# Second power and first inverse step in one product, and token products of one head as transposes, in a chunked RWKV-7 recurrence

## What is computed

```python
def step(state, inp):
    r_t, w_t, k_t, v_t, kk_t, a_t = inp
    sa = jnp.einsum('bhvk,bhk->bhv', state, -kk_t)
    state = (state * w_t[:, :, None, :]
             + sa[..., None] * (kk_t * a_t)[:, :, None, :]
             + v_t[..., None] * k_t[:, :, None, :])
    return state, jnp.einsum('bhvk,bhk->bhv', state, r_t)
s0 = jnp.zeros((bsz, RWKV_HEADS, RWKV_HEAD_DIM, RWKV_HEAD_DIM), f32)
_, y = lax.scan(step, s0, tuple(map(seq_first, (r, decay, k, v, kk, a))))
```

## Time and profile before

| | |
|---|---|
| median of 3 runs | 2763.23 us (2763.11 to 2765.14) |
| profiled execution | 2771.98 us, of which the span is 2770.1 us |
| the stage `rwkv` on TensorE | about 1214.5 to 1765 us |
| granted clock of TensorE, mean | 0.986 of full |

### The profile page before, as it was taken

The page is one execution under the profiler, slowest core; times in us unless marked ns, Lnnn a source line. Parts: engine busy times, 40 slices in busy tenths (PEclk is TensorE's granted clock), DMA queues, the critical chain, the costliest instruction groups (busy, mean ns, idle before and its releaser), DMA issues. The chain is left out here.

```text
span 2770.1 us, 66149 instructions
## 1 busy us (share of the span) xinstructions
PE 2617.0 (94%) x28073; PEld 2190.7 (79%) x28073; DVE 1563.2 (56%) x2377; ACT 1318.0 (48%) x2272; POOL 316.2 (11%) x367
## 2 busy tenths in 40 slices
PE   6999999999999999989999999999999999999992
PEld 5989897777766766678999998888888888888882
DVE  4566664443035555544444444553326888888884
ACT  4645552222134444334444444552223777777771
POOL 0111222332000000001212121100001000000002
PEclk9999999999999999999999999999998999999996
DMA  4344332222132323313221201154345999999976
GB/s 111 148 167 145 125 138 89 92 93 74 37 96 65 99 68 102 114 38 81 55 69 52 64 21 33 48 152 129 121 185 219 397 395 395 395 396 395 395 301 258
DMA packets 162649, 440.53 MB, mean 159 GB/s; under 512 B 16295, under 2 KB 96825, under 8 KB 150097
## 3 DMA queue, kind: packets, MB, share of 16 engines
q1 hardware_dynamic: 146413, 381.95, 38.7%
q10 hardware_dynamic: 9060, 29.56, 2.8%
q0 software_dynamic: 6912, 25.17, 2.4%
HBM read 344.22 MB, written 92.41 MB: 158 GB/s over the span
## 5 line engine op out<-in xcount | busy, mean ns | idle before, releaser
L2671 DVE TENSOR_TENSOR ex_wL<-wx,ex_wH 128x2048 fp32r<-128x2048 f32 x192 | 436.1, 2286 | 46.5 <-ACT ex_wH L2575 43.8
L2575 ACT CAST ex_wH<-wx 128x2048 fp32r<-128x2048 f32 x192 | 366.4, 1912 | 96.3 <-PE ex_bank L2467 70.7
L2465 PE MATMUL ex_bank<-ex_wH,ex_xTH 128*128 128x512 f32 x512 | 199.4, 389 | 0.6 <-DVE ex_xTL L2676 0.6
L2467 PE MATMUL ex_bank<-ex_wL,ex_xTH 128*128 128x512 f32 x512 | 199.3, 389 | 0.0
L2466 PE MATMUL ex_bank<-ex_wH,ex_xTL 128*128 128x512 f32 x512 | 199.2, 389 | 0.0
L717 PE MATMUL ph_acc<-ph_wH,uH 128*104 128x512 f32 x480 | 191.5, 399 | 0.0
L717 PE MATMUL ph_acc<-ph_wH,uL 128*104 128x512 f32 x480 | 188.8, 393 | 0.0
L717 PE MATMUL ph_acc<-ph_wL,uH 128*104 128x512 f32 x480 | 188.6, 393 | 0.0
L419 PE MATMUL pf_acc<-uH,pf_wH 128*128 128x348 f32 x648 | 160.7, 356 | 6.4 <-DVE pf_wL L541 6.4
L419 PE MATMUL pf_acc<-uL,pf_wH 128*128 128x348 f32 x648 | 138.9, 323 | 0.0
L419 PE MATMUL pf_acc<-uH,pf_wL 128*128 128x348 f32 x648 | 138.3, 322 | 0.0
(11 more groups left out here) (416 smaller groups left out, 6879.5 us busy)
## 6 DMA issues: line engine op xcount, KB each, us to landing
wx<-in_expert_w_gate SPq DMA_DIRECT2D x32, 2048.0 KB
wx<-in_expert_w_up SPq DMA_DIRECT2D x32, 2048.0 KB
wx<-in_expert_w_down SPq DMA_DIRECT2D x32, 2048.0 KB
s_y<-ex_y ACTq DMA_DIRECT2D x32, 512.0 KB, 10.0
fw<-in_w_in SPq DMA_DIRECT2D x27, 512.0 KB
hw<-in_w_in SPq DMA_DIRECT2D x6, 2048.0 KB, 10.1
s_qkT<-ph_stg ACTq DMA_DIRECT2D x4, 2080.0 KB, 7.0
mb_gt<-s_pT SPq DMA_DIRECT2D x16, 512.0 KB, 3.6
```

The costliest lines, as they stand in the source:

```text
L2465: nc.tensor.matmul(out, aH, bH, start=first, stop=False)
L2467: return nc.tensor.matmul(out, aH, bL, start=False, stop=last)
L2575: nc.scalar.copy(wH[:, w, part], raw(j, s)[:, part]).then_inc(w_high, 1)
L2671: nc.vector.tensor_tensor(wL[:, w, part], raw(j, s)[:, part], wH[:, w, part], ALU.subtract).then_inc(w_low, 1)
```

## The change

Step 7 no longer issues the product with Q0 on its own. GpSimd writes its sum into the new middle place of `X2`, next to the second power, and one product with a moving operand twice as wide (104 columns) gives the next power and the product with the first factor, both into bank `bx`. ScalarE copies X4 from that bank as before, from columns 0 to 4 TC; VectorE's sum of step 7 reads columns 4 TC to 6 TC of the same bank and, new, waits for ScalarE's copy. GpSimd's sum waits for the step-7 sum of two chunks before instead of four. Of the token products those of the lower head (`h` = 0) are issued as transposes; those of the upper head stay.

```diff
-        X2 = sb("rw_X2", [128, 2, 2, 2, TC])
+        X2 = sb("rw_X2", [128, 2, 3, 2, TC])
...
-        Q0 = sb("rw_Q0", [128, TS4, 2, TC])
...
                 elif n == 7:
                     pe.wait_ge(*at_act(ch, 6))
                     pe.wait_ge(*at_pool(ch, 6))
+                    both = lambda e, h: bank[here(h), bx, 0:8 * TC].rearrange("p (k r t) -> p k r t", k=2, r=4)[:, :, e, :]
                     for e in range(2):
                         for h in range(2):
-                            mm(at(bx, 0, e, h), X2[here(h), ln, 1, e, :], X2[here(h), ln, 0, e, :], start=True, stop=True)
+                            mm(both(e, h), X2[here(h), ln, 2, e, :], X2[here(h), ln, 0:2, e, :], start=True, stop=True)
                         for h in range(2):
-                            mm(at(bx, 1, e, h), X2[here(h), ln, 0, e, :], X2[here(h), ln, 1, e, :], start=True, stop=True)
-                        for h in range(2):
-                            last = mm(at(bq, 0, e, h), X2[here(h), ln, 1, e, :], Q0[here(h), f, e, :], start=True, stop=True)
+                            last = mm(at(bx, 1, e, h), X2[here(h), ln, 0, e, :], X2[here(h), ln, 2, e, :], start=True, stop=True)
...
-                        last = mm(bank[here(h), 7, (2 * j + e) * RD:(2 * j + e + 1) * RD], src, c.ident[half(h), half(h)], start=True, stop=True)
+                        if h == 0:
+                            last = tr(bank[here(h), 7, (2 * j + e) * RD:(2 * j + e + 1) * RD], src, c.ident[half(h), half(h)])
+                        else:
+                            last = mm(bank[here(h), 7, (2 * j + e) * RD:(2 * j + e + 1) * RD], src, c.ident[half(h), half(h)], start=True, stop=True)
...
-                what = {6: (X2[0:PX, ln], four), 7: (X4[0:PX, ln], four), 8: (N8[0:PX, ln], two),
+                what = {6: (X2[0:PX, ln, 0::2], four), 7: (X4[0:PX, ln], four), 8: (N8[0:PX, ln], two),
...
-            for b, n in ((2, 4 * TC), (3, 2 * TC), (4, 4 * TC), (5, 2 * TC)):
+            for b, n in ((2, 6 * TC), (3, 2 * TC), (4, 6 * TC), (5, 2 * TC)):
...
-                    if ch >= TS4:
-                        pool.wait_ge(*at_dve(ch - TS4, 7))
-                    nc.gpsimd.tensor_tensor(Q0[0:PX, ch % TS4], M4[0:PX, ch % MS, :, 0, :], eye, ALU.add).then_inc(spool[ln], 1)
+                    if ch >= 2:
+                        pool.wait_ge(*at_dve(ch - 2, 7))
+                    nc.gpsimd.tensor_tensor(X2[0:PX, ln, 1], M4[0:PX, ch % MS, :, 0, :], eye, ALU.add).then_inc(spool[ln], 1)
...
                     if n == 7:
                         dve.wait_ge(*at_pool(ch, 6))
+                        dve.wait_ge(*at_act(ch, 7))
...
-                    tt(dst, pairs(bq), Q0[0:PX, ch % TS4] if n == 7 else Q[0:PX, ln, 1 - n % 2], ALU.add).then_inc(sdve[ln], 1)
+                    src = bank[0:PX, bx, 4 * TC:6 * TC].rearrange("p (e t) -> p e t", e=2) if n == 7 else pairs(bq)
+                    tt(dst, src, X2[0:PX, ln, 1] if n == 7 else Q[0:PX, ln, 1 - n % 2], ALU.add).then_inc(sdve[ln], 1)
```

## The result

The changed kernel takes 2913.05 us (median of 4 runs, 2906.97 to 2918.09) against 2764.18 us before: ratio 1.053, 95% interval 1.050 to 1.056. It is 149 us slower; 2743 us had been predicted. The profiled execution took 2918.09 us.

A forecast was written before the change was run, and what follows sets the result against it. The supply of TensorE's instructions was taken to bound two thirds of the stage. Fewer instructions -24.1, waits there +2.2, the other third +2.5: -19.4 us, taken as -20, from 2763.2 to 2743 us; likeliest case 2733 to 2751, range 2733 to 2768.

The forecast's parts named there:

- What bounds the kernel: In two thirds of the recurrence stage, TensorE's instruction supply: about 256 instructions per 3.97 us, against 3.54 us of work.
- the terms: Fewer TensorE instructions: 14 records a chunk, -24.1 us, of which step 7's eight give 13.8; array time adds 0.7 us.
- no supply bound: Rival: the "issue" gaps are a fixed toll per piece of instructions; +5.2 us, 2768 us; chance 0.13.
- Token products: Six of twelve products a chunk become transposes; a pair still takes 0.112 us, so array time saved is taken as zero.
- drain: Rival: each of 480 token transposes takes the array out of its quarters and back; +114 us, 2877 us; chance 0.07.
- The rule that I cited: On TensorE, a change of tiling mode drains it, and column tiling excludes float32 transposes; time as under drain, 2877 us.
- Serial: Rival: token transpose and product take turns on the array, 27 us of work; -4 us, 2759 us; chance 0.14 (or half).
- The new wait: VectorE's step-7 sum waits for ScalarE's X4 copy; step 8 0.12 us late, 10.0 us in all, mostly hidden by supply.
- The clock: In the recurrence stage, read at its full level of 2.4 GHz; the sum had no term for a change.

The follow-up runs named there:

- step7_order: Kernel before with the new step 7, token products as before, all waits kept but the one that ends last written first: 2758.08 us, ratio 0.9960.
- tokens_only: Kernel before with only the lower head's token products turned into transposes, step 7 unchanged: 2893.94 us, ratio 1.049.
- masked_split: Kernel before with each masked product of 104 columns issued as two of 52, 16 records a chunk more: 2789.28 us, ratio 1.0111.
- tokens_grouped: Kernel before with the lower head's token products as transposes, six in a row, then the upper head's six products: 2776.86 us, ratio 1.0038.
- the grouped runs: Kernel before with the lower head's token products as transposes, six or two in a row, then as many upper-head products: 2776.86 and 2810.26 us.

## Why the prediction was wrong

**What bounds the kernel** was read rightly. The supply of TensorE's instructions in pieces of 256 costs time: 16 records more a chunk gave +31 us where 30 were expected, and eight fewer, with no late wait, gave -16 where the terms make -14.5. The rival "no supply bound" falls.

**Token products** is the step that failed: "Array time saved: nothing", and the cost taken at nothing beyond it. Its direct term measured +138 us. The rival "drain" had the mechanism and the price: 0.306 us for each transpose, against 0.30 measured, from the norm's transposes of the earlier trace rows. I held it at 0.07 because the transposes into 16 partitions follow full-size ones without a toll. Those rows were the wrong witness: no product in a quarter stands near them, and what costs is the change between products in quarters and a transpose, in a quarter or full-size, which the earlier trace rows alone showed. The rule that I cited from the Trainium skill (TensorEngine Tiling (Array Packing), Key Properties and Restrictions) pointed the right way: the trace agrees that a change costs, 0.24 to 0.27 us for in and out. What the array does in that time no run shows. That the norm's transposes gave nearly the same price, 0.25 us, is read and not explained. "Serial" falls too.

**The new wait** was right as a mechanism and mis-sized: step 8 is 0.32 us late, not 0.12 (0.35 from start to start, less 0.03). Two sizes were wrong in it, the hand-offs of 0.03 and 0.06 us, which measured 0.131 and 0.146. The rows from which I took the hand-offs were of instructions on which the wait that ended last was the only one or the first written; the change puts it last at both ends. With that put right (step7_order), the prediction's 0.12 to 0.15 us late in most chunks and 10.0 us in all hold: 0.13 us in 68 chunks, 9 us in all.

**The clock** was not in the sum at all: full speed was taken for granted since the stage had it before. It measured about 27 us.

The stage of after in terms: +138 for the token blocks, -38 for the gaps, +27 with the clock, which is tokens_only's 127 us; from there to 146 are 19 us for the new step 7 with its late step 8 (0.32 us x the 61 times that the list of waits has, 20 us, less some array time). It is an account and not a proof: the starts of after give the clock 17 us without the ends of the stage, and the execution of before that was profiled lies 8 us above its median. The rival "drain" had forecast +114 us: its -41 for the gaps and its 147 for the transposes came about; it lacked the clock and had half the wait.

## What to carry to other kernels

Before one operation in an interleaved pattern is put in another form, look for a row in which the two forms stand next to each other (here products in quarters and a transpose; among full-size products a transpose was free), and multiply the toll of one change by the number of changes: a saved record is worth 0.024 us here (31 us over the 1,280 of masked_split), a change of form and back 0.25 us. If the forms have to be mixed, put one kind in a row. Where an instruction waits for several semaphores, write the one that ends last first, or drop those that it implies; and where the profile names "issue" at a place that repeats in every chunk, look whether a wait on a semaphore instruction stands behind it.

## What was not expected of the hardware

- A wait that ends last on a semaphore instruction of its own costs 0.10 us (VectorE) and 0.09 us (TensorE) more than the same wait on the working instruction, though the semaphore instruction itself shows 0.05 us. The profile gives it as "issue".
- A transpose of 64x52 float32 starts 0.056 us behind the last one (tokens_grouped), but 0.14 to 0.15 us behind a product in quarters; a product in quarters starts 0.146 us behind it in the grouped runs and 0.167 us in tokens_only, where the two alternate.
- Full-size float32 transposes follow full-size products at the products' own distance (0.112 us, 47 of 48 places in before), while behind products in quarters they start 0.146 us on.
- The granted clock falls to half in a stage in which TensorE shows 99% busy (670.90 of 677.50 us in tokens_only). Busy is not progress: at full clock too a pair's records cover the 0.41 us in which two starts of a product and one of a transpose fall. Which part of the pattern brings the fall was not isolated: three groups a chunk don't, six do.
